# The first block's rotary halves swapped by ScalarE's row copies in place of a matrix product on TensorE

## The reference

```python
def apply_rope(u, cos, sin):
    u1, u2 = jnp.split(u.astype(jnp.float32), 2, axis=-1)
    return jnp.concatenate([u1 * cos - u2 * sin, u2 * cos + u1 * sin], axis=-1)
...
for l in range(DEPTH):
    h = rms_norm(x, norm_g[l])
    (q, k_c, v_c, k_s, v_s, k_w, v_w, g_lin, z_nsa, ...) = jnp.split(h @ w_in[l], split_points(), axis=-1)
    q, k_c, k_s, k_w = (apply_rope(a, cos, sin) for a in (q, k_c, k_s, k_w))
    y_nsa = nsa_attention(q, k_c, v_c, k_s, v_s, k_w, v_w, gates, cmp_pos[l], cmp_w1[l], cmp_w2[l])
    ...
```

## Time and profile before

| | us |
|---|---|
| median of 3 runs | 2240.78 |
| the runs | 2235.54 to 2242.61 |
| profiled execution, its own time | 2239.98 |
| its span in the profile | 2238.2 |
| TensorE busy | 2156.2 (96%) |
| VectorE busy | 1194.8 (53%) |
| ScalarE busy | 1013.7 (45%) |
| GpSimd busy | 1013.6 (45%) |

### The profile page before, as it was taken

How to read it: one execution, slowest core, us unless ns; L and a number is a source line. 1 busy time by engine, 2 the same in 40 slices (tenths; PEclk the granted TensorE clock), 3 DMA queues, 4 the chain that set the end, 5 groups by cost and what they waited for, 6 DMA issues and landing times.

```text
span 2238.2 us, 32910 instructions
## 1 busy us (share of the span) xinstructions
PE 2156.2 (96%) x11928; PEld 1751.0 (78%) x11928; DVE 1194.8 (53%) x2502; ACT 1013.7 (45%) x2020; POOL 1013.6 (45%) x921
## 2 busy tenths in 40 slices
PE   8999889999998899999999999999989999999997
PEld 6778667887876788777888888888767878888886
DVE  6997774389776645785562202234466654211222
ACT  6542465465245643485463323343356544322332
POOL 4433445444335443364345545554345525545553
PEclk9999989999998999999999999999999999999999
DMA  5334002333310233202323333334120413333331
GB/s 172 89 92 136 23 11 74 102 93 90 123 62 2 59 98 94 86 21 75 96 81 99 94 109 97 93 98 126 45 62 25 131 49 101 98 93 100 99 93 67
DMA packets 106895, 187.87 MB, mean 84 GB/s; under 512 B 12016, under 2 KB 22768, under 8 KB 106608
## 3 DMA queue, kind: packets, MB, share of 16 engines
q1 hardware_dynamic: 101136, 178.67, 27.4%
q10 hardware_dynamic: 5600, 7.11, 1.0%
HBM read 181.01 MB, written 2.10 MB: 82 GB/s over the span
## 4 chain that ended last, share of the span: by engine, by line
PE 86%; DVE 7%; issue 2%; ACT 2%; POOL 1%; DMA 0%; SPq 0%; DVEq 0%; ACTq 0%
PE bank L945 24%; PE bank L947 23%; PE bank L946 23%; PE bank L1183 4%; PE bank L1196 3%; PE bank L1163 3%; DVE bank L2236 1%; PE bank L952 1%; PE bank L1015 1%; PE bank L1142 1%; ACT temp L1524 1%; POOL temp L2396 1%; PE bank L1064 1%; DVE temp L2073 0%; POOL w_lo L2438 0%
## 5 line engine op out<-in xcount | busy, mean ns | idle before, releaser
L2438 POOL TENSOR_TENSOR w_lo<-w_raw,w_hi 128x512 fp32r<-128x512 f32 (+3 forms) x618 | 824.2, 1339 | 975.3 <-ACT w_hi L1329 975.0
L945 PE MATMUL bank<-op_hi,w_hi 128*128 128x512 f32 x1840 | 733.5, 399 | 10.7 <-POOL w_lo L2438 4.2
L947 PE MATMUL bank<-op_hi,w_lo 128*128 128x512 f32 x1840 | 719.1, 391 | 0.0
L946 PE MATMUL bank<-op_lo,w_hi 128*128 128x512 f32 x1840 | 718.8, 391 | 0.0
L1329 ACT ACTIVATE w_hi<-w_raw 128x512 fp32r<-128x512 f32 (+2 forms) x634 | 385.3, 617 | 685.0 <-PE bank L947 681.6
L945 PEld LDWEIGHTS bank<-op_hi,w_hi 128*128 128x128 f32 x1840 | 346.9, 189 | 95.1 <-issue 15.4
L946 PEld LDWEIGHTS bank<-op_lo,w_hi 128*128 128x128 f32 x1840 | 347.2, 189 | 74.2 <-issue 4.6
L947 PEld LDWEIGHTS bank<-op_hi,w_lo 128*128 128x128 f32 x1840 | 346.8, 188 | 73.5
L1768 DVE TENSOR_TENSOR temp<-bank,rstd 128x512 f32<-128x512 f32 x139 | 96.1, 691 | 369.2 <-PE bank L947 350.3
L945 PE MATMUL bank<-side_hi,w_hi 128*128 128x512 f32 (+1 forms) x628 | 233.1, 371 | 2.6 <-DVE side_lo L1867 1.4
L947 PE MATMUL bank<-side_hi,w_lo 128*128 128x512 f32 (+1 forms) x628 | 230.9, 368 | 0.0
(11 more groups left out here) (286 smaller groups left out, 2444.3 us busy)
## 6 DMA issues: line engine op xcount, KB each, us to landing
w_raw<-in_weights SPq DMA_DIRECT2D x620, 256.0 KB, 2.7
w_raw<-in_weights SPq DMA_DIRECT2D x32, 192.0 KB, 2.3
temp<-temp SPq DMA_DIRECT2D x40, 64.0 KB, 2.0
x_t<-in_x SPq DMA_DIRECT2D x8, 256.0 KB, 4.9
conv_area<-in_mem ACTq DMA_DIRECT2D x2, 1024.0 KB, 5.4
conv_area<-in_bias ACTq DMA_DIRECT2D x1, 2048.0 KB, 7.5
out_y<-ybuf SPq DMA_DIRECT2D x8, 256.0 KB, 2.1
w_raw<-in_weights SPq DMA_DIRECT2D x10, 128.0 KB, 2.2
```

The costliest lines, as they stand in the source:

```text
L945: pe.matmul(dst, w[0], m[0], start=start, stop=False)
L946: pe.matmul(dst, w[0], m[1], start=False, stop=False)
L947: return pe.matmul(dst, w[1], m[0], start=False, stop=stop)
L2438: pool.tensor_tensor(w_lo[:, j, 0:n], w_raw[:, p % RAW_RING, 0:n], w_hi[:, j, 0:n].bitcast(F32), ALU.subtract).then_inc(*mark("weights_spl ...
```

## The change

TensorE no longer multiplies by `rot` in part B. Instead ScalarE copies, in `evac(n)` of the strip itself, blocks of 32 rows of `RAW(n)` to the swapped place in a second buffer, `swapped[u % 2]` (u numbers the rotated strips): four copies of 32x512 for a strip, two of them with scale -1. The copies wait for VectorE's evacuation of the strip and for the sum of the rotated strip but one before. VectorE waits for them by a new semaphore, `rows_swapped`, and multiplies by the sine in place in that buffer instead of reading bank 3. The matrix `rot` leaves the constants.

```diff
@@ rope_units(s)
-                return [(C("rot") if s.kind == "q" else None, s.idx)]
+                return [("rows" if s.kind == "q" else None, s.idx)]
...
@@ TensorE, rotate(n)
-                    if rot is None:
+                    if rot is None or s.part[0] == "B":
                         continue
@@ ScalarE, evac(n)
+                elif k in ("q", "k_s", "k_w", "k_c"):
+
+                    u = s.units[0]
+                    act.wait_ge(*after("strip_taken", n))
+                    if u >= 2 and UNITS[u - 2][0] == "rows":
+                        act.wait_ge(*after("roped", u - 2))
+                    for a in range(0, P, HD):
+                        act.activation(swapped[u % 2][a:a + 32, :], RAW(n)[a + 32:a + HD, :], ACT.Copy, scale=-1.0)
+                        ins = act.activation(swapped[u % 2][a + 32:a + HD, :], RAW(n)[a:a + 32, :], ACT.Copy)
+                    ins.then_inc(*mark("rows_swapped", u))
@@ VectorE, rope(n)
-                    src, swap = RAW(n), UNITS[u][0] is None
-                    dve.wait_ge(*after(f"swapped{u % 2}" if swap else "rotated", u))
+                    by_rows = s.part[0] == "B"
+                    src, swap = RAW(n), UNITS[u][0] is None or by_rows
+                    dve.wait_ge(*after("rows_swapped" if by_rows else f"swapped{u % 2}" if swap else "rotated", u))
```

More of the change, by code:

```diff
@@ L213 @@
 N_PARAM = _at
-CONSTS = [("ident", P), ("ones", P), ("halves", P), ("rot", P), ("causal", T), ("cmp_mask", NT * CMP_PAD), ("cmp_any", 1), ("inv_freq", 1)]
+CONSTS = [("ident", P), ("ones", P), ("halves", P), ("causal", T), ("cmp_mask", NT * CMP_PAD), ("cmp_any", 1), ("inv_freq", 1)]
 EXTRA = [("rotc", P), ("band", 384), ("cos2d", T), ("sin2d", T), ("cos1d", T), ("sin1d", T), ("cosc", T), ("sinc", T),
@@ L518, in rope_units @@
             if s.kind in ("q", "qn"):
-                return [(C("rot") if s.kind == "q" else None, s.idx)]
+                return [("rows" if s.kind == "q" else None, s.idx)]
             if s.kind in ("k_s", "kn"):
-                return [(C("rot") if s.kind == "k_s" else None, 4)]
+                return [("rows" if s.kind == "k_s" else None, 4)]
             if s.kind in ("qr", "kr"):
@@ L524, in rope_units @@
             if s.kind == "k_w":
-                return [(C("rot"), 5)]
+                return [("rows", 5)]
             if s.kind == "k_c":
-                return [(C("rot"), "cmp")]
+                return [("rows", "cmp")]
             if s.kind == "uq":
@@ L2459, in shape_constants @@
     swap_sign = np.where(d % HD < 32, -1, 1).astype(f)[:, None]
-    rot = np.zeros((P, P), f)
-    for o in range(P):
-        rot[o + 32 if o % HD < 32 else o - 32, o] = -1 if o % HD < 32 else 1
     q, x = d[:, None], np.arange(T)[None, :]
@@ L2467, in shape_constants @@
         ident=np.eye(P, dtype=f), ones=np.ones((P, P), f), halves=(d[:, None] // HD == d[None, :] // HD).astype(f),
-        rot=rot,
         causal=np.where(x - 384 <= q, 0, NEG).astype(f),
```

## The result

| | before | after |
|---|---|---|
| median, us | 2238.16 | 2263.05 |
| the four runs, us | 2235.18 to 2242.61 | 2260.97 to 2264.98 |
| span of the profiled execution, us | 2238.2 | 2260.0 |
| ratio to before, 95% interval | | 1.0108 [1.0091, 1.0125] |

The change costs 24.9 us (2263.05 less 2238.16). The prediction added 6.1 and 4.6, so 10.7, and said 2251.5, range 2244 to 2259. Two executions of later kernels fell far outside (12103.73 us of e4, 3549.07 us of e9): they are counted in those medians and left out of the ratios.

What follows compares the result with a forecast made beforehand. The prediction took TensorE, busy 96%, to bound the kernel: 2239.98 + 6.1 (late starts) + 4.6 (lower clock) = 2250.7 us, and with 0.8 us for the median 2251.5 us, range 2244 to 2259.

Steps and rivals of the forecast that it cites:

- What bounds the kernel: Whole kernel: TensorE, busy 96%, bounds it alone; a second chain through q2's weights, ending at TensorE, is nearly as long.
- The 12 us of products: Part B, TensorE: 14 removed products at 0.85 to 0.88 us each, about 12 us, the whole gain to be had.
- The rival in which the gain comes through: Part B: splits ready early or 32-row copies at 0.13 us, so products come back; 2229 to 2234 us, chance 0.08.
- Where the copies stand: ScalarE's in-order queue: q3's split waits behind q2's copies and v_s's behind k_s's, two places a layer.
- The pitch of a copy: ScalarE's 32x512 copies: pitch 0.52 us, 2.2 us a strip, 29 us in all; bounds 0.13 and 0.72.
- the fixed path: From a strip's evacuation start through copies, split and low part to the next strip's first matmul: 4.97 us.
- k_c, q0, q1: Start of part B: k_c's copies delay VectorE, its slack absorbs part; q2 starts 0.2 us later in the first layer.
- VectorE reads SBUF in place of PSUM, so nothing: VectorE's L1985: reading SBUF instead of PSUM costs nothing, since rows of both sorts take 0.69 us.
- The stalls' sum: Part B, late strip starts at full clock: +3.37 us in the first layer, +2.77 in the second, together +6.1 us.
- The clock: Part B, lower TensorE clock behind idle stretches: three stretches counted, +4.6 us; bounds 0 to 8.
- three signs named for a wrong prediction: Splits for q3 or v_s starting before copies end, much shorter 32-row copies, or clock staying 1.00 behind idle stretches.
- "dearer" rival: Part B: copies at 0.72 us, clock falling four or five times; 2257 us, up to 2260, chance 0.17.

Runs made afterwards that it cites:

- e4: Kernel after with matmuls of constants into an unused bank on TensorE ahead of q2, q3 and v_s, to fill idle stretches; 2254.19 us, ratio 1.0063.
- e9: Kernel after with the four copies written into PSUM bank 3 instead of the SBUF buffers; 2264.34 us, ratio 1.0116.
- e13: Kernel e5 (no products, no copies) with the earlier splits of e2 in part B; 2238.02 us, ratio 0.9999.
- e5: Kernel after with the copies deleted too, so neither products nor copies, halves not swapped; 2242.48 us, ratio 1.0014.
- e1: Kernel after with a strip's copies moved to the next strip's turn, behind its first split; 2251.41 us, ratio 1.0053.
- e2: Kernel e1 with an earlier split of strip n+2's weights added in every turn of part B; 2239.20 us, ratio 1.0002.
- e6: Kernel before, products kept, plus the four copies at the change's place into a buffer nothing reads; 2264.38 us, ratio 1.0113.
- e12: Kernel after with GpSimd's subtraction replaced by a copy of w_raw in the first layer's part B, second layer unchanged; 2258.70 us, one run.
- e7: Kernel after with each group of four ScalarE copies in another form (rows, columns, shift, SBUF or PSUM), none making the swap; 2251.47 us, one run.

## Why the prediction was wrong, step by step

- **What bounds the kernel.** "What leaves TensorE's queue should come back, unless TensorE then waits" was half right. The second chain was seen, but as one from weights to TensorE. That VectorE's own work fills the time from k_c to q2's evacuation, never waiting for TensorE (e13), was not. The 12 us of products, "the whole gain to be had", came to nothing in e5 and e13: VectorE's chain took most of them, and the lower clock behind the waits took the rest and, in e5, more. The rival in which the gain comes through had no case at this place of the copies, whatever their pitch, since with no copies at all (e5) nothing came.
- **Where the copies stand.** Right. q3's split ran behind q2's copies (179.55), v_s's behind k_s's, and moving them took the loss back (e1, e2); e6 shows the loss with the products still in place.
- **The pitch of a copy.** Taken 0.52, measured 0.64, so the fixed path from evacuation to first matmul is 181.67 - 176.25 = 5.42 us, not 4.97. The bounds of 0.13 and 0.72 held. It costs 0.44 us at q3 and again at v_s.
- **k_c, q0, q1: the step whose mechanism failed.** Predicted 0.2 us for q2, measured, counted from k_c's evacuation, 167.72 - 146.05 = 21.67 against 18.95: 2.7 us. In the second layer it is +1.7 where -0.4 was predicted. The copies at 0.64 give 0.4 more at k_c and again at q1; L2001 and L2003 beside GpSimd took 3.48 in place of L1990 and L1992's 1.03 and 0.69 before, 1.76 more; VectorE then had no slack left. "VectorE reads SBUF in place of PSUM, so nothing" was too quick: the change also moved those instructions beside GpSimd's w_lo.
- **The stalls' sum.** Predicted starts +0.20, +1.08, +4.26 at q2, q3, v_s; measured, the clock's share taken out, +2.72, +4.04, +7.66. From q2 on each step grows by the predicted amount and 0.44. At z0 the products saved at d1 leave +6.8, and +5.8 in the second layer: 12.6 in place of 6.1.
- **The clock: the term mis-sized most.** Right in kind, 4.6 predicted, 12.4 measured. Five strips lost it, as the upper bound had it, but each lost 2.1 to 2.7 us and not 1.5. No run shows the sum's 4.6, which is three stretches of 1.5; in its place after lost 12.4 in its five strips, and the kernels of the table 4.9 to 12.4 where any was lost. The 1.5 is what the strip behind 2.52 us of idle lost in part A of before: its 24 matmuls took 39.54 - 32.45 = 7.09 us, 1.55 beyond 5.54. The lower level stayed longer in part B: for some 5.8 us at q2, where the strip in part A had eight matmuls at 0.50. The same 2.01 us of idle at q3 cost 2.55 us in the first layer, 5.7 us behind the slow q2, and nothing in the second, so the length of one idle stretch did not decide it.
- **Sum.** 6.1 + 4.6 became 12.6 + 12.4. Of the 14.3 us that were missing, 7.8 are the clock, 4.6 the start of q2 in both layers, and 1.9 the pitch of the copies ahead of q3 and v_s. None of the three signs named for a wrong prediction came up: its mechanism at q3 and v_s held, its prices and the step at q2 did not. The "dearer" rival had the right parts, but took them as a price of the copies, and stopped at 2260.

## To carry to other kernels

A busy share of 96% does not say that work removed comes back. Measure the next chain by itself, best with a kernel that leaves the work out and puts nothing in its place, and read the clock in it too: here it came out no faster (1.0014), in part because the holes cost 8.0 us of clock. Work added in an in-order queue costs what stands behind it: 56 copies of 0.64 us on an engine that is 45% busy cost 25 us at one place and nothing at another. Before moving GpSimd's work, look for what VectorE does beside it with two SBUF operands: here 1.66 to 1.82 us in place of 0.69.

## What the hardware showed that I had not expected

- A VectorE instruction on 128x512 fp32 with both inputs in SBUF takes 0.69 us alone. Wholly beside a GpSimd subtraction the multiplications by the cosines take mostly 1.64 to 1.82, those by the sines mostly 1.12 to 1.45 (after, e2); beside a GpSimd copy it is about 1.0 to 1.1 (e12). With one input in PSUM it stays at 0.68 or 0.69 beside the subtraction (e9). GpSimd's own pair rises from 2.56 to 2.99 us (after).
- ScalarE's copies overlap with their neighbour (pitch 0.21 for 0.29 at 128 columns, e7) on the same rows, and not when the rows change (0.64 for 0.63 at 512 columns, after).
- Behind 5.22 us of idle the granted clock was 0.50 for 3.30 us and 0.75 on average over the next 4.99. In shorter windows of after it was 0.50 up to 173.00, 0.60 from there to 173.60 and 1.00 from 173.60 on, so some 5.8 of q2's 8.3 us ran at 0.50. Behind 2.52 us in part A the lower clock cost 1.5 us (7.09 less 5.54). In e13 a strip behind only 0.94 us of idle took 7.17 us in place of 5.54. The stalls of the kernel after, filled with matmuls of constants (e4), left it at 1.00.
